# First sum of squares between the interleaved recurrent products, gate products one block ahead, first down output added next to the eviction

## What is computed

```python
def rglru_mixer(x, h0, conv_buf, positions, w_in, conv_w, conv_b, w_a, b_a, w_x, b_x, lam, w_out):
    u = x @ w_in
    gate_branch, rec = u[..., :D_RNN], u[..., D_RNN:]
    xc = causal_dwconv(x_full, conv_w, conv_b)
    r = jax.nn.sigmoid(block_diag(xc, w_a, b_a).astype(jnp.float32))
    i = jax.nn.sigmoid(block_diag(xc, w_x, b_x).astype(jnp.float32))
    log_a = -RG_C * r * jax.nn.softplus(-lam.astype(jnp.float32))
    ...
    y = (h.astype(x.dtype) * jax.nn.gelu(gate_branch)) @ w_out
def conv_ffn(x, buf, w_up, conv_w, conv_b, w_down):
    u = x @ w_up
    uc = causal_dwconv(u_full, conv_w, conv_b)
    val, gate = uc[..., :D_FF], uc[..., D_FF:]
    return (jax.nn.gelu(gate) * val) @ w_down, new_buf
```

## Time and profile before

| what | us |
|---|---|
| median of 3 runs | 2788.56 |
| lowest, highest | 2787.03, 2793.2 |
| the profiled execution | 2785.28 |
| its span in the trace, first to last instruction | 2783.5 |
| PE busy in the span | 2670.1 (96%) |
| DVE, ACT, POOL busy | 1426.9, 684.4, 839.5 |

### The profile page before, as it was taken

One profiled execution on the slowest core, in us unless ns is written; L12 is line 12 of the kernel. 1 busy time (PEld: TensorE's weight loads), 2 busy tenths in 40 slices (PEclk: granted clock), 3 DMA queues, 4 the chain that ended last, 5 costly groups with the idle time before them and its releaser, 6 DMA issues.

```text
span 2783.5 us, 39635 instructions
## 1 busy us (share of the span) xinstructions
PE 2670.1 (96%) x16596; PEld 2586.7 (93%) x16596; DVE 1426.9 (51%) x2220; ACT 684.4 (25%) x1127; POOL 839.5 (30%) x473
## 2 busy tenths in 40 slices
PE   5999999999999999989999999799999999999995
PEld 4999999999999999978888889699999999999995
DVE  6666365444444444474444444536544444444446
ACT  4445131111111111133444444513111111111111
POOL 2342333332333333334333332022333333233231
PEclk8999999999999999989999999899999999999998
DMA  3111311111111111123222222311111111111111
GB/s 131 35 50 31 116 39 45 46 46 46 46 46 46 46 46 46 51 104 122 78 86 86 86 91 79 146 44 46 46 44 42 45 46 46 46 46 46 46 46 69
DMA packets 78672, 170.51 MB, mean 61 GB/s; under 512 B 9333, under 2 KB 44149, under 8 KB 78238
## 3 DMA queue, kind: packets, MB, share of 16 engines
q1 hardware_dynamic: 71442, 140.02, 15.5%
q10 hardware_dynamic: 7052, 27.96, 2.7%
HBM read 145.91 MB, written 26.76 MB: 62 GB/s over the span
## 4 chain that ended last, share of the span: by engine, by line
PE 87%; DVE 7%; ACT 3%; issue 2%; POOL 1%; ACTq 0%; DVEq 0%; POOLq 0%
PE psum L714 69%; PE psum L856 4%; PE psum L860 3%; PE psum L858 3%; PE psum L909 2%; PE psum L885 2%; DVE line L1448 2%; DVE x L1513 2%; PE psum L897 1%; ACT line L1215 1%; PE psum L935 1%; PE psum L961 1%; DVE line L1489 1%; POOL w_lo L606 1%; DVE inverse_rms L1501 0%
## 5 line engine op out<-in xcount | busy, mean ns | idle before, releaser
L714 PE MATMUL psum<-xn_hi,w_hi 128*128 128x352 f32 x3120 | 679.6, 326 | 32.0 <-DVE xn_lo L1495 13.9
L714 PE MATMUL psum<-xn_lo,w_hi 128*128 128x352 f32 x3120 | 675.1, 324 | 0.0
L714 PE MATMUL psum<-xn_hi,w_lo 128*128 128x352 f32 x3120 | 674.0, 324 | 0.0
L602 POOL TENSOR_SCALAR w_hi<-w_raw 128x1024 fp32r<-128x1024 f32 x176 | 189.9, 1079 | 1512.5 <-PE psum L714 1499.5
L714 PEld LDWEIGHTS psum<-xn_hi,w_hi 128*128 128x128 f32 x3120 | 533.8, 190 | 35.9 <-issue 21.9
L714 PEld LDWEIGHTS psum<-xn_lo,w_hi 128*128 128x128 f32 x3120 | 538.1, 189 | 0.0
L714 PEld LDWEIGHTS psum<-xn_hi,w_lo 128*128 128x128 f32 x3120 | 532.1, 188 | 0.0
L606 POOL TENSOR_TENSOR w_lo<-w_raw,w_hi 128x1024 fp32r<-128x1024 f32 x176 | 453.6, 2577 | 14.7
L1215 ACT ACTIVATE line<-line,columns 128x1072 f32<-128x1072 f32 x96 | 123.4, 1285 | 1062.3 <-DVE line L1471 1062.3
L1513 DVE TENSOR_TENSOR x<-psum,x 128x1056 f32<-128x1056 f32 x208 | 261.2, 1256 | 227.7 <-PE psum L714 226.9
L1466 DVE TENSOR_TENSOR line<-psum,inverse_rms 128x704 f32<-128x704 f32 x104 | 92.8, 892 | 472.0 <-PE psum L714 471.9
(11 more groups left out here) (213 smaller groups left out, 2691.4 us busy)
## 6 DMA issues: line engine op xcount, KB each, us to landing
w_raw<-in_w SPq DMA_DIRECT2D x200, 512.0 KB, 3.5
k_pages<-in_cache_k SPq DMA_DIRECT2D x128, 64.0 KB, 1.9
v_pages<-in_cache_v SPq DMA_DIRECT2D x128, 64.0 KB, 1.9
scratch_line<-scratch_row ACTq DMA_DIRECT2D x1, 4608.0 KB, 21.3
x<-in_x ACTq DMA_DIRECT2D x8, 528.0 KB, 10.9
scratch_x<-x ACTq DMA_DIRECT2D x1, 4224.0 KB, 12.1
out_k<-raw ACTq DMA_DIRECT2D x8, 528.0 KB, 3.2
out_v<-raw ACTq DMA_DIRECT2D x8, 528.0 KB, 3.1
```

What stands on the lines that cost most here:

```text
L602: pool.tensor_scalar(WHI[:, s], WRAW[:, s], 1.0, 0.0, ALU.mult, ALU.add).then_inc(w_hi, 1)
L714: last = pe.matmul(PS[:, 3 * (a % 2) + c, 0:CH], w[:, s, k, :], r[:, c * CH:(c + 1) * CH], start=start and first, stop=stop and final)
```

## The change

It has three parts.

1. **Sum of squares.** The helper `norm_sum` is cut into `norm_prompt` (the sums over the prompt) and `norm_samples`. In the stage of the two interleaved products, the first stands behind the sixth of eight steps, the second behind the seventh, where both stood behind the eighth.
2. **Gate products one block ahead.** Gate product 0 is made before `diag(0)`, and turn n of the loop makes gate product n - 1 and not n - 2. The order on PE becomes gate 0, diag 0, rec 2, gate 1, diag 1, rec 3, gate 2, and so on, and at the end rec 7, diag 6, gate 6, diag 7, gate 7. All numberings, SP's loads, POOL's splits and ACT's order follow. On DVE `gated_y` is moved behind the scan, so that it stands just ahead of `xc_low`, and `rec(n)` is cut into `rec_in` (eviction) and `rec_conv`.
3. **First down output.** In the FFN the first down output is added between the eviction of the last up product and the wait for its tap, and no more between `conv_first` and `conv_last`.

```diff
 def acc_rec(n):
-    return n if n < 2 else 4 * n - 4
+    return n if n < 2 else 4 * n - 3
 def acc_gate(n):
-    return 4 * n + 5 if n < 6 else (28, 31)[n - 6]
+    return 4 * n + 2 if n < 6 else (28, 31)[n - 6]
@@ PE
+                if k == KT - 3:
+                    norm_prompt(0)
+                if k == KT - 2:
+                    norm_samples(0)
+            pe.wait_ge(root_done, 2)
             bias_line()
+            unit(unit_gate(0), acc_gate(0))
             diag(0)
-            for n in range(2, KT):
+            for n in range(2, KT - 1):
                 unit(unit_rec(n), acc_rec(n))
-                unit(unit_gate(n - 2), acc_gate(n - 2))
+                unit(unit_gate(n - 1), acc_gate(n - 1))
                 diag(n - 1)
+            unit(unit_rec(KT - 1), acc_rec(KT - 1))
+            diag(KT - 2)
             unit(unit_gate(KT - 2), acc_gate(KT - 2))
             diag(KT - 1)
@@ ACT
-            for n in range(2, KT):
+            for n in range(2, KT - 1):
                 tap(n)
-                gelu(n - 2)
+                gelu(n - 1)
                 recurrence(n - 1)
                 xc_high(n)
@@ DVE
-            for n in range(2, KT):
-                rec(n)
-                gate(n - 2)
-                gated_y(n - 2)
+            for n in range(2, KT - 1):
+                rec_in(n)
+                rec_conv(n)
+                gate(n - 1)
                 input_gate(n - 1)
                 scan(n - 1)
+                gated_y(n - 1)
                 xc_low(n)
+            rec_in(KT - 1)
+            rec_conv(KT - 1)
+            input_gate(KT - 2)
+            xc_low(KT - 1)
             gate(KT - 2)
+            scan(KT - 2)
             gated_y(KT - 2)
@@ DVE, FFN group
                     arrived(g, 1, 1, i)
+                    outs(0, 1)
+                    tapped(g, 1, 1, i)
                     w = taps(g, 1, 1, i)
                     conv_first(Z[5], TMP[1], w, None, FW - 1)
-                    outs(0, 1)
                     conv_last(Z[5], TMP[1], Z[1], w, FW - 1, q["gc_ready"])
```

More of the change, by code:

```diff
@@ L86, in acc_rec @@
 def acc_rec(n):
-    return n if n < 2 else 4 * n - 4
+    return n if n < 2 else 4 * n - 3
 def acc_gate(n):
-    return 4 * n + 5 if n < 6 else (28, 31)[n - 6]
+    return 4 * n + 2 if n < 6 else (28, 31)[n - 6]
 def acc_diag(n):
-    return 2 if n == 0 else 4 * n + 2 if n < 7 else 29
+    return 4 * n + 3 if n < 6 else (26, 29)[n - 6]
 def unit_rec(n):
-    return n if n < 2 else 2 * n - 2
+    return n if n < 2 else 2 * n - 1
 def unit_gate(n):
-    return 2 * n + 3 if n < 6 else n + 8
+    return 2 * n + 2 if n < 6 else n + 8
 def accs_after():
@@ L496, in _ @@
             for n in range(2, KT):
+                pairs(unit_gate(n - 2), unit_gate(n - 2) + 1)
                 pairs(unit_rec(n), unit_rec(n) + 1)
                 load_gates(n)
-                pairs(unit_gate(n - 2), unit_gate(n - 2) + 1)
             pairs(unit_gate(KT - 2), U_OUT)
@@ L642, in _ @@
             for n in range(2, KT):
+                straight(unit_gate(n - 2), unit_gate(n - 2) + 1)
                 straight(unit_rec(n), unit_rec(n) + 1)
                 gates(n - 1)
-                straight(unit_gate(n - 2), unit_gate(n - 2) + 1)
+            straight(unit_gate(KT - 2), unit_gate(KT - 2) + 1)
             gates(KT - 1)
-            straight(unit_gate(KT - 2), U_OUT)
+            straight(unit_gate(KT - 1), U_OUT)
             straight(U_OUT, U_OUT + 2)
@@ L735, in norm_sum, with norm_prompt @@
             def norm_sum(r):
+                norm_prompt(r)
+                norm_samples(r)
+                pe.wait_ge(root_done, 2 * r + 2)
+            def norm_prompt(r):
                 pe.wait_ge(sum_done, KT * (r + 1))
@@ L741, in norm_sum, with norm_samples @@
                           ).then_inc(sum_mm, 1)
+            def norm_samples(r):
                 pe.wait_ge(root_done, 2 * r + 1)
@@ L744, in norm_sum @@
                           ).then_inc(sum_mm, 1)
-                pe.wait_ge(root_done, 2 * r + 2)
             def bias_line():
@@ L776, in _ @@
                         last.then_inc(acc_done, 1)
-            norm_sum(0)
+                if k == KT - 3:
[3 more added lines that the diff above has]
+            pe.wait_ge(root_done, 2)
             bias_line()
+            unit(unit_gate(0), acc_gate(0))
             diag(0)
-            for n in range(2, KT):
+            for n in range(2, KT - 1):
                 unit(unit_rec(n), acc_rec(n))
-                unit(unit_gate(n - 2), acc_gate(n - 2))
+                unit(unit_gate(n - 1), acc_gate(n - 1))
                 diag(n - 1)
+            unit(unit_rec(KT - 1), acc_rec(KT - 1))
+            diag(KT - 2)
             unit(unit_gate(KT - 2), acc_gate(KT - 2))
@@ L1167, in _ @@
             tap(1)
+            gelu(0)
             recurrence(0)
             xc_high(1)
-            for n in range(2, KT):
+            for n in range(2, KT - 1):
                 tap(n)
-                gelu(n - 2)
+                gelu(n - 1)
                 recurrence(n - 1)
                 xc_high(n)
+            tap(KT - 1)
+            recurrence(KT - 2)
+            xc_high(KT - 1)
             gelu(KT - 2)
@@ L1560, in _, with rec_in, rec_conv @@
             REC, TI, SQ, A_, S_, G_ = Z[4], Z[1], Z[2], Z[3], Z[6], Z[5]
-            def rec(n):
-                XC = XCS[n % 2]
+            def rec_in(n):
                 dve.wait_ge(rec_used, n + 1)
                 evac_line(acc_rec(n), REC, RW - 1)
+            def rec_conv(n):
+                XC = XCS[n % 2]
                 dve.wait_ge(rec_tap, n + 1)
@@ L1618, in y_low @@
                                   ).then_inc(nlo_done, 1)
-            rec(0)
+            rec_in(0)
+            rec_conv(0)
             xc_low(0)
-            rec(1)
+            rec_in(1)
+            gate(0)
+            rec_conv(1)
             input_gate(0)
             scan(0)
+            gated_y(0)
             xc_low(1)
-            for n in range(2, KT):
-                rec(n)
-                gate(n - 2)
-                gated_y(n - 2)
+            for n in range(2, KT - 1):
+                rec_in(n)
+                rec_conv(n)
+                gate(n - 1)
                 input_gate(n - 1)
                 scan(n - 1)
+                gated_y(n - 1)
                 xc_low(n)
+            rec_in(KT - 1)
+            rec_conv(KT - 1)
+            input_gate(KT - 2)
+            xc_low(KT - 1)
             gate(KT - 2)
+            scan(KT - 2)
             gated_y(KT - 2)
@@ L1677, in arrived, with tapped @@
                     evac_line(a, Z[4 + v], FW - 1, i, 24)
-                    dve.wait_ge(q["tap_done"], val(n + 1, i, 8))
+                def tapped(g, t, v, i):
+                    dve.wait_ge(q["tap_done"], val(2 * (2 * g + t) + v + 1, i, 8))
                     f = 2 * g + t
@@ L1697, in convolved @@
                     arrived(g, t, v, i)
+                    tapped(g, t, v, i)
                     w = taps(g, t, v, i)
```

## The result

The changed kernel takes 2801.06 us (median of 5 runs, 2799.37 to 2802.44) beside 2788.56 before (five runs): a ratio of 1.0040 with an interval of 1.0026 to 1.0055. It is slower by 12.5 us; 2799.5 was forecast, with 2784 to 2808 as the range. The profiled execution has a span of 2797.6 us, 14.1 more than the 2783.5 before.

What follows compares the result with a forecast made beforehand. PE, busy 96% of the span, was taken as the bound, with DVE and POOL holding each other up. Recurrent stage +21, FFNs -11 and clock +1 gave +11 on 2788.56: 2799.5 us, range 2784 to 2808.

Steps and rivals of the forecast that it cites:

- head start, restart of PE: Ahead of the recurrent loop: PE makes gate product 0 in idle time and restarts at 67.4 instead of 68.18, -0.8 us.
- five turns: Recurrent loop, between the tanh of blocks 0 and 5: each turn 4.6 us longer, 31.8 instead of 27.2, +23.0 us.
- to gate product 6: End of the loop, from the tanh of block 5 to gate product 6: 28.8 us instead of 28.5, +0.3.
- gate 6 to the third output product: End of the stage: diag 7 loses its wait and low clock, -4.5 us; late high and low parts of y, +3.
- FFNs: Both FFNs: PE's wait at the third down output goes, 0.5 us in each of 22 groups, -11 us.
- rest, clock: Whole kernel: PE's low clock in the new gaps costs +1 us (0 to 5).
- the clock may be low or high in 46 to 50: Front, at gate product 0: PE's clock level left open, worth up to 1.7 us.
- both collisions: Loop turn: POOL's w_lo gets ahead of xc_low, 3.4 us later; POOL's splits around the last convolution step, gate evicted 4.6 late.
- it is the same walk in each turn: Recurrent loop: all five turns lose the same 4.6 us, since POOL's and DVE's steps both hang on the last tanh.
- Rival B: Loop: second collision slips through, gate evicted 2.4 us late, not 4.6; 11 less, 2788.5, no change; chance 0.15.
- Rival C: Loop: collisions cost nothing, turns stay at 27.2 us; -17 in all, 2771.5, faster; chance 0.12.
- rival D: FFN: the wait only moves to the fourth down output, -2 us instead of -11, 2808.5; chance 0.08.

Runs made afterwards that it cites:

- own-line experiment: Changed kernel with gated_y in the tap's gap, turn 7 made like the others, recurrence 7's second tanh given its own line, scan 6 later: 2769.15 us, ratio 0.9926.
- before_y_ahead: Kernel before with one line moved, gated_y(n - 2) behind the scan and ahead of xc_low(n): 2813.38 us, ratio 1.0084.

## Why the prediction was right, and where only its sum was

The sign, the mechanism and the total held: 2799.5 forecast, 2801.06 measured, the stage +21 forecast and +21.1 in the trace. The mechanism is shown: the move of gated_y alone makes the kernel before slower by 23 us, and its move to another place takes the cost of the loop away. The terms held less well. Each term by the rows; of before these are the first tanh (ACT) and PE's restart at gate product 6:

```profile
66.89 1.14 ACT L1144 ACTIVATE line<-psum,half_b_a 128x1056 f32<-128x1056 f32 x1
...
204.33 1.13 ACT L1144 ACTIVATE line<-psum,half_b_a 128x1056 f32<-128x1056 f32 x1
```

```profile
232.80 0.72 PE L714 MATMUL psum<-xn_hi,w_hi 128*128 128x352 f32 x3 [0.52 <-POOL w_lo L606]
```

and of after the tanh (ACT):

```profile
68.20 1.14 ACT L1159 ACTIVATE line<-psum,half_b_a 128x1056 f32<-128x1056 f32 x1 [5.30 <-DVE xc L1474]
97.93 1.12 ACT L1159 ACTIVATE line<-psum,half_b_a 128x1056 f32<-128x1056 f32 x1
129.54 1.12 ACT L1159 ACTIVATE line<-psum,half_b_a 128x1056 f32<-128x1056 f32 x1
160.10 1.12 ACT L1159 ACTIVATE line<-psum,half_b_a 128x1056 f32<-128x1056 f32 x1
188.41 1.12 ACT L1159 ACTIVATE line<-psum,half_b_a 128x1056 f32<-128x1056 f32 x1
220.03 1.12 ACT L1159 ACTIVATE line<-psum,half_b_a 128x1056 f32<-128x1056 f32 x1
```

| term | forecast | measured | from |
|---|---|---|---|
| head start, restart of PE | -0.8 | +1.3 | 69.48, 68.18 |
| five turns | +23.0 | +14.4 | 220.03 - 68.20 = 151.8, 204.33 - 66.89 = 137.4 |
| to gate product 6 | +0.3 | +1.8 | 250.28 - 220.03, 232.80 - 204.33 |
| gate 6 to the third output product | -4.5 + 3 | +3.6 | 312.92 - 250.28, 291.84 - 232.80 |
| stage | +21 | +21.1 | |
| FFNs | -11 | -10.5 | below |
| rest, clock | +1 | +3.5 | 14.1 - 21.1 + 10.5 |

**The front.** The early steps came out to 0.1: sums at 32.81 (forecast 32.8), reciprocal at 38.14 (38.25), gate product 0 at 46.47 (46.5). Its eviction was at 60.52 and not 58.3. The step that was short is "the clock may be low or high in 46 to 50": the stretch from 46 to 61 shows a mean clock of 0.83. From the end of that eviction to the end of the convolution it was 6.3 us (forecast 6.45), POOL's w_lo among it: the pair of steps took 4.92 instead of 2.72.

**The loop.** The walk of a turn held to 0.2 us where both collisions take place: 31.61 and 31.62, against 31.8. The step that failed is "it is the same walk in each turn". It is not, because PE's new gap makes PE come back at the low level; the next product ends later, POOL's split, which waits for it, starts later, and meets another operation of DVE. From the first tanh to the first w_hi of the turn it is 13.25 in the second turn, 14.52 in the third, behind the groups of 1.25 and 1.08 at 128.57, and 14.35 in the fourth, behind the 1.22 at 161.36. In the third turn w_hi came 0.20 behind the last convolution step (155.72, 155.52), which then took 1.28, and only the samples' step had to wait for it (30.56). In the fourth it missed gated_y too (28.31); DVE and POOL there:

```profile
174.38 1.26 DVE L1608 TENSOR_TENSOR y<-y,line 128x1056 f32<-128x1056 f32 x1
174.45 2.10 POOL L602 TENSOR_SCALAR w_hi<-w_raw 128x1024 fp32r<-128x1024 f32 x1 [14.28 <-PE psum L715]
175.56 2.09 DVE L1597 TENSOR_TENSOR xc_lo<-line,xc_hi 128x1056 fp32r<-128x1056 f32 x1
```

w_hi is 0.07 behind gated_y instead of ahead of it, so only w_hi and not w_lo lies between the two. Rival B (about 29.5) had the second collision slip through in every turn; that came true in this one alone. Rival C, no cost, is out by every kernel with gated_y in this place. The first turn (29.73 for 28.68) was counted as a full one, though it has no collision of either kind: w_hi (83.97) comes behind gated_y (82.47) and beside xc_low, which takes 1.25, and the eviction of the gate product waits 2.79 for PE.

One reading of the rows was wrong and changed nothing: w_lo's 2.40 in the earlier trace rows is not beside line 1513, which starts at 604.91, when w_lo had ended at 603.75. That an operation of DVE that reads PSUM and w_lo pass each other is shown by the row at 157.80 instead.

**The end.** Here the forecast was too kind by 6.6 us. It put PE's two gaps at "some 6.5" each (5.65 and 4.07 measured) and their clock at nothing, under the +1 of the sum. From 250.28 the first seven groups take 6.0 us, where 0.485 each would be 3.4, and from 284.99 six take 5.3 for 2.9. The granted clock of this stretch, after and then before:

```profile
220.00:313.00 93.00, 75.85 (x405) 74.22 (x403) 53.20 (x59) 41.83 (x39) 15.77 (x11) 0.86 0.17 55
```

```profile
205.00:292.00 87.00, 78.52 (x470) 77.10 (x470) 54.15 (x61) 43.41 (x40) 24.13 (x14) 0.98 0.22 66
```

And the "+3" for the high and low parts of y was 4.74: they stand behind recurrence 7, whose second tanh waited 5.61 us for scan 6, a wait that the forecast did not have. The own-line experiment takes just this wait away and keeps the gain.

**The FFN.** The addition moved as forecast, and the convolution step behind it takes 1.33 (forecast 1.34, not 1.90); the groups keep their pace of 0.485. DVE and POOL:

```profile
622.91 2.41 POOL L606 TENSOR_TENSOR w_lo<-w_raw,w_hi 128x1024 fp32r<-128x1024 f32 x1
...
624.63 1.26 DVE L1532 TENSOR_TENSOR x<-psum,x 128x1056 f32<-128x1056 f32 x1 [1.46 <-PE psum L715]
625.80 1.33 DVE L1467 SCALAR_TENSOR_TENSOR line<-line,columns,line 128x1072 f32<-128x1072 f32 x1
```

The tap of the first up product starts at 408.76 (385.82 before), that of the last at 2718.70 (2703.88). The lag falls from 22.9 to 14.8, though 2.3 are lost between the FFNs (17.7 at the last tap of the first FFN, 20.1 at the first of the second): 10.5 won, 0.48 a group. The convolution step takes 1.32 or 1.33 in all 22 groups, so rival D is out.

**Right by what?** The loop was 8.6 too dear, the front, the end, the FFNs and the rest together 11.7 too cheap. The low clock behind the gaps was summed as +1, where 5 us were lost at the two restarts of the end alone. The forecast's hit to 1.6 us (3.1 between the two traces) is partly the luck of terms that cancel; the sign is not.

## What to carry to other kernels

Before an operation of VectorE is moved, look at what GpSimd does beside it in its old and in its new place: an SBUF-only operation that used to start 0.02 us ahead of GpSimd's can cost the length of GpSimd's whole operation once another one stands ahead of it (3.45 us for 1.26), and one that reads PSUM costs nothing there (1.25). A head start on PE is worth what is left at the end of the stage, so follow it to the last restart. And count each new gap of PE twice, as a wait and as the work behind it that runs at the lower level.

## What the hardware showed that was not expected

Which of DVE and POOL is there first decides between 0.25, 1.03 and 2.32 us for an operation of 32 columns: 2.32 where w_hi started 0.01 us ahead of the convolution step in front of it, 1.03 where it came 0.20 behind that. With gated_y ahead of xc_low, xc_low came out at 3.45 or 3.46 in all five turns of before_y_ahead. The runs of one kernel lie 12 us apart (before: 2785 to 2797), the slower ones at the lower mean clock (2797 at 0.975, 2785 to 2787 at 0.979), which is as much as this change is worth. The times have a standard deviation of 3.4 us, time x clock one of 1.5: it separates kernels better than the time does where their gaps are alike.
